# First layer's tokens come turned, and their 1/rms is applied behind the projections

## What is computed

```python
def _rms_norm(x, g):
    y = xf * lax.rsqrt(jnp.mean(xf * xf, axis=-1, keepdims=True) + NORM_EPS)
    return (y * g.astype(jnp.float32)).astype(x.dtype)

h = _rms_norm(x, norm_mix)
proj = h @ w_in                       # 1024 x 3336
rq, rk, rv, rg, fq, fk, fv, fl, cb, cc, ch = jnp.split(proj, split_at, axis=-1)
# A: retention: rotary on rq, rk; values rv; group norm and swish gate rg
# B: forgetting attention: RMS norm of each head of fq, fk; logf = log_sigmoid(fl + bias)
u = cc * ch
y_conv, new_conv = _causal_dwconv(u, conv_hist, conv_w)
o_conv = (cb * y_conv).astype(x.dtype)
x = x + jnp.concatenate([o_ret, o_fox, o_conv], axis=-1) @ w_out
h2 = _rms_norm(x, norm_ffn)
x = x + (jax.nn.silu(gate_c) * (h2 @ w_up)) @ w_down
```

## Time and profile before

| | us |
|---|---|
| Median of 3 runs | 1559.53 (1558.76 to 1560.35) |
| Span of the profiled execution | 1557.5 |
| PE busy | 1538.9 |
| DVE busy | 1056.6 |
| ACT busy | 661.2 |
| POOL busy | 408.5 |
| First 128x512 product of the projections | at 11.58 |
| First forget-gate matmul (end of chunk 0) | at 45.20 |

### The profile page before, as it was taken

The page is one execution under the profiler, slowest core; times in us unless marked ns, Lnnn a source line. Parts: engine busy times, 40 slices in busy tenths (PEclk is TensorE's granted clock), DMA queues, the critical chain, the costliest instruction groups (busy, mean ns, idle before and its releaser), DMA issues.

```text
span 1557.5 us, 28313 instructions
## 1 busy us (share of the span) xinstructions
PE 1538.9 (99%) x9860; PEld 1343.1 (86%) x9860; DVE 1056.6 (68%) x1805; ACT 661.2 (42%) x1236; POOL 408.5 (26%) x513
## 2 busy tenths in 40 slices
PE   8999999999999999999999999999999999999998
PEld 6878896789999999999888788867899999999997
DVE  4446447449988788888644563574599887888885
ACT  4223337336544444444333133373364444444441
POOL 1113210004433333333112041100145333333330
PEclk9999999999999999999999999999999999999999
DMA  7213436531322222222242235465223222222222
GB/s 235 82 49 94 140 122 239 211 95 55 108 82 85 85 85 83 85 88 68 80 109 68 71 85 168 145 235 178 68 90 100 81 81 81 81 81 81 81 69 85
DMA packets 116971, 163.80 MB, mean 105 GB/s; under 512 B 28049, under 2 KB 80401, under 8 KB 112802
## 3 DMA queue, kind: packets, MB, share of 16 engines
q1 hardware_dynamic: 116752, 162.75, 33.1%
q10 hardware_dynamic: 146, 0.07, 0.0%
HBM read 152.91 MB, written 9.63 MB: 104 GB/s over the span
## 4 chain that ended last, share of the span: by engine, by line
PE 93%; DVE 3%; ACT 1%; DMA 1%; issue 1%; POOL 0%; POOLq 0%; DVEq 0%; SPq 0%; ACTq 0%
PE bank L2233 89%; PE bank L2295 4%; DVE pf L1884 0%; DMA raw<-in_w_gate 0%; DVE pf L1897 0%; DVE xn L1572 0%; DMA raw<-in_w_in 0%; DVE x L2008 0%; DVE wlo L1534 0%; POOLq L1110 0%; POOL s L1108 0%; DVE gulo L1544 0%; ACT xn L1216 0%; POOL small L978 0%; DVE xlo L1534 0%
## 5 line engine op out<-in xcount | busy, mean ns | idle before, releaser
L2233 PE MATMUL bank<-whi,hhi 128*128 128x512 f32 x560 | 226.0, 404 | 0.9 <-DVE hlo L1544 0.6
L2233 PE MATMUL bank<-whi,hlo 128*128 128x512 f32 x560 | 219.4, 392 | 0.0
L2233 PE MATMUL bank<-wlo,hhi 128*128 128x512 f32 x560 | 219.0, 391 | 0.0
L2233 PE MATMUL bank<-hhi,whi 128*128 128x320 f32 x640 | 198.7, 310 | 0.8 <-DVE hlo L1544 0.8
L2233 PE MATMUL bank<-hhi,wlo 128*128 128x320 f32 x640 | 197.8, 309 | 0.0
L2233 PE MATMUL bank<-hlo,whi 128*128 128x320 f32 x640 | 197.6, 309 | 0.0
L2233 PE MATMUL bank<-whi,guhi 128*128 128x512 f32 x440 | 171.9, 391 | 0.2
L2233 PE MATMUL bank<-wlo,guhi 128*128 128x512 f32 x440 | 171.3, 389 | 0.0
L2233 PE MATMUL bank<-whi,gulo 128*128 128x512 f32 x440 | 171.3, 389 | 0.0
L1520 DVE TENSOR_TENSOR wlo<-raw,whi 128x1024 fp32r<-128x1024 f32 x80 | 100.1, 1251 | 99.7 <-ACT whi L1143 98.1
L2008 DVE TENSOR_TENSOR x<-x,bank 128x512 f32<-128x512 f32 x220 | 142.8, 681 | 29.6 <-PE bank L2233 29.2
(11 more groups left out here) (307 smaller groups left out, 3500.6 us busy)
## 6 DMA issues: line engine op xcount, KB each, us to landing
raw<-in_w_in SPq DMA_DIRECT2D x52, 512.0 KB, 3.8
raw<-in_w_gate SPq DMA_DIRECT2D x44, 512.0 KB, 3.8
raw<-in_w_down SPq DMA_DIRECT2D x44, 512.0 KB, 3.6
raw<-in_w_up SPq DMA_DIRECT2D x24, 512.0 KB, 3.8
vb<-in_cache_fox_v SPq DMA_DIRECT2D x10, 1024.0 KB, 5.5
gains<-in_w_up SPq DMA_DIRECT2D x20, 512.0 KB, 3.7
raw<-in_w_out SPq DMA_DIRECT2D x16, 512.0 KB, 4.6
bcr<-scr_p SPq DMA_DIRECT2D x8, 512.0 KB, 5.0
```

Of the source, the lines that this page charges most:

```text
L2233: return pe.matmul(out, lhsT=lhsT, rhs=rhs, start=start, stop=stop, skip_group_check=True)
```

## The change

In layer 0 the host also gives the tokens turned (`x_turned`, with the first layer's gain in eight columns ahead). ACT rounds x^T times the gain straight into `hhi` (`hi(k)`), DVE makes the rest (`rest(k)`), for k = 0 to 7, with 640 tokens in each. There is no norm and no transpose ahead of the products; slab 0 is used by row, k = 0 for all tiles, then k = 1, and its two halves are loaded by ACT's queue. The row sums and 1/rms are made afterwards from x, which is loaded later. The 1/rms of a token is then applied where the projections are read: as the scale of ACT's copies and Silu, on the rotary's cos and sin, on the forget values, through the epsilon of the head norms (`FLOOR`), and for the turned branch (cc, ch, cb) as a row `rb`, which SP sends through DRAM (`scr_r`) to all partitions: POOL multiplies cc with its square and y with itself. Layer 1 runs as before. The diff, cut:

```diff
+        rb = own("rb", [P, NTOK])
+        (xt, fqT, fkT, fv, h11, h12, guhi, gulo, gact, t2h, t2l, s1, s2) = region(
+            [("xt", [P, XT], F32)],
...
-            load_x(sp, 0)
-            sp.dma_start(const[:, 0:P], a["c_tables"][:, 0:P]).then_inc(ident_in, 16)
...
-                    sp.wait_ge(lo_split, nth(n, l))
+                    if l > 0 or n >= SLOTS:
...
+            def load_xt(i):
+                c0, c1 = (KT + NTOK * k if k else 0 for k in XT_PARTS[i:i + 2])
+                sp.dma_start(xt[:, c0:c1], a["x_turned"][:, c0:c1]).then_inc(xt_in[i], 16)
+
+            load_xt(0)
+            load_xt(1)
+            load(1, 0, slab_src(1, 0))
+            load_xt(2)
+            load(2, 0, slab_src(2, 0))
+            load_xt(3)
+            load_xt(4)
+            load(SLOTS, 0, slab_src(SLOTS, 0))
+            sp.dma_start(const[:, :], a["c_tables"]).then_inc(consts_in, 16)
...
+                if l == 0:
+                    for t in range(3):
+                        load_x(sp, t)
...
+                if l == 0:
+                    sp.wait_ge(rstd, TT)
+                    sp.dma_start(scr_r.rearrange("t p -> p t"), small[:, RS:RS + TT], allow_slow_non_contiguous=True).then_inc(r_out, 16)
+                    sp.wait_ge(r_out, 16)
+                    sp.dma_start(rb[:, :], bass.AP(scr_r.tensor, 0, [[0, P], [1, NTOK]])).then_inc(rb_in, 16)
 
...
+            turned_before = [sum(1 for t in range(TT) for g in range(2) if B.bank(("hT", 0, t, g)) == b) for b in range(8)]
             for b in range(8):
-                pool.sem_inc(B.free[b], 1)
+                pool.sem_inc(B.free[b], 1 + turned_before[b])
+                if turned_before[b]:
+                    pool.sem_inc(B.full[b], turned_before[b])
+            pool.sem_inc(h_hi, 2 * TT)
+            pool.sem_inc(xn_ready, TT)
             pool.sem_inc(lo_split, SLOTS)
             pool.sem_inc(x_done, 2 * TT)
...
+                    if l == 0 and which == 0:
+                        pool.tensor_scalar(col(FLOOR + t), col(VAR + t), EPS, 0.0, ALU.mult, ALU.add)
...
+                if l == 0:
+                    pool.wait_ge(rb_in, 16)
+                    pool.tensor_tensor(rb2[:, :], rb[:, :], rb[:, :], ALU.mult)
+                    pool.drain()
...
+                for i in range(4) if l == 0 else ():
+                    ft, half = i // 2, i % 2
+                    hs = slice(half * HALF, half * HALF + HALF)
+                    B.wait_taken(pool, ("cc_", ft, half), l)
+                    pool.tensor_tensor(ccs[:, ft, hs], ccs[:, ft, hs], rb2[:, hs], ALU.mult).then_inc(cc_scaled, 1)
...
+                for ft in range(2) if l == 0 else ():
+                    pool.wait_ge(y_conv, ft + 1)
+                    apart(pool)
+                    pool.tensor_tensor(ycv[:, ft, 0:SEQ], ycv[:, ft, 0:SEQ], rb[:, 0:SEQ], ALU.mult)
+                    rows = ycv[:, ft, NY - NB * (NS + 2):NY].rearrange("p (b s) -> p b s", b=NB)[:, :, 2:]
+                    pool.tensor_tensor(rows, rows, rb[:, SEQ:].rearrange("p (b s) -> p b s", b=NB), ALU.mult)
+                    pool.drain().then_inc(y_scaled, 1)
...
-            act.dma_start(vb[0:1, 0, 0:2, :].rearrange("p k n -> p (k n)"), a["norm_mix"][bass.ds(0, 1)]).then_inc(gains_in, 16)
+            def turned_tokens(l):
+
+                def hi(k):
+                    if k in XT_PARTS:
+                        act.wait_ge(xt_in[XT_PARTS.index(k)], 16)
+                    act.activation(hhi[:, k, :], xt[:, KT + NTOK * k:KT + NTOK * (k + 1)], ACT.Copy,
+                                   scale=xt[:, k:k + 1]).then_inc(xt_hi, 1)
+
+                hi(0)
+                act.wait_ge(w_first_in, 16)
+                act.activation(whi[:, 0, 0:512], raw[:, 0, 0:512], ACT.Copy).then_inc(w_first_hi, 1)
+                hi(1)
+                wait_loaded(act, 0, l)
+                act.activation(whi[:, 0, 512:], raw[:, 0, 512:], ACT.Copy).then_inc(hi_split, 1)
+                split_to[0] = 1
+                upto(1, l)
+                hi(2)
+                hi(3)
+                upto(2, l)
+                for k in range(4, KT):
+                    hi(k)
+                upto(3, l)
+
+            def token_squares():
+                for t in range(TT):
+                    act.wait_ge(x_in[t], 16)
+                    if t >= 2:
+                        act.wait_ge(rstd, t - 1)
+                    act.activation(rT[:, 2 * (t % 2):2 * (t % 2) + 2, 0:512], x[:, t, :].rearrange("p (c n) -> p c n", c=2), ACT.Square,
+                                   accum_out=col(SS + t)).then_inc(sumsq, 1)
+                    if t == 1:
+                        upto(FL, 0)
+                    if t == 2:
+                        upto(FL + 1, 0)
+
+            for k, done in ((0, w_first_in), (1, raw_in[0])):
+                act.dma_start(raw[:, 0, 512 * k:512 * k + 512].rearrange("p (k n) -> p k n", k=1),
+                              a["w_in"][bass.ds(0, 1)].rearrange("o (k p) n -> p (o k) n", p=P)[:, k:k + 1, 0:512]).then_inc(done, 16)
...
-                norm(0, l, {0: 0, 1: 2} if l == 0 else {0: 0, 2: 1, 3: 2})
+                if l == 0:
+                    turned_tokens(l)
+                    token_squares()
+                else:
+                    norm(0, l, {0: 0, 2: 1, 3: 2})
...
+                    act.activation(gs[:, t, :], bk[:, 256:512], ACT.Silu, scale=token_scale(t)).then_inc(silu_ready, 1)
+                    act.activation(rv[:, t, :], bk[:, 0:256], ACT.Copy, scale=token_scale(t)).then_inc(B.free[B.bank(("c", 1, t))], 1)
...
-            dve.wait_ge(gains_spread, 1)
-            dve.tensor_copy(gains[:, 0:512], bank[6][:, :])
-            dve.drain()
-            dve.wait_ge(ident_in, 16)
+            def turned_tokens(l):
+
+                def rest(k):
+                    dve.wait_ge(xt_hi, k + 1)
+                    dve.scalar_tensor_tensor(out=hlo[:, k, :], in0=xt[:, KT + NTOK * k:KT + NTOK * (k + 1)], scalar=xt[:, k:k + 1],
+                                             in1=hhi[:, k, :].bitcast(F32), op0=ALU.mult, op1=ALU.subtract).then_inc(xt_lo, 1)
+
+                rest(0)
+                dve.wait_ge(w_first_hi, 1)
+                lo(wlo[:, 0, 0:512], raw[:, 0, 0:512], whi[:, 0, 0:512]).then_inc(w_first_lo, 1)
+                rest(1)
+                dve.wait_ge(hi_split, 1)
+                lo(wlo[:, 0, 512:], raw[:, 0, 512:], whi[:, 0, 512:]).then_inc(lo_split, 1)
+                split_to[0] = 1
+                upto(1, l)
+                rest(2)
+                rest(3)
+                upto(2, l)
+                for k in range(4, KT):
+                    rest(k)
...
+                    csr = cs[:, t]
+                    if l == 0:
+                        dve.wait_ge(rstd, t + 1)
+                        csr = wcn[:, 64 * (t % 2):64 * (t % 2) + 64].rearrange("p (s d) -> p s d", s=2)
+                        dve.tensor_scalar(csr, cs[:, t], col(RS + t), None, ALU.mult)
...
-                    B.wait_taken(dve, ("cc_", i // 2, i % 2), l)
+                    if l == 0:
+                        dve.wait_ge(cc_scaled, i + 1)
+                    else:
+                        B.wait_taken(dve, ("cc_", i // 2, i % 2), l)
...
                 def conv_times(ft, half):
                     key = ("cb_", ft, half)
+                    if l == 0:
+                        dve.wait_ge(y_scaled, ft + 1)
...
-            pe.wait_ge(gains_in, 16)
-            for c in range(2):
-                mm(bank[6 + c][:, :], ob[0:1, 0, :], vb[0:1, 0, c, :], True, True).then_inc(gains_spread, 1)
-            pe.wait_ge(ident_in, 16)
...
+                def slab_by_row():
+                    pe.wait_ge(w_first_lo, 1)
+                    for k in range(2):
+                        pe.wait_ge(xt_lo, k + 1)
+                        if k == 1:
+                            ready(0, l)
+                        for t in range(TT):
+                            key, ts = ("c", 0, t), slice(t * P, t * P + P)
+                            if k == 0:
+                                B.wait_room(pe, key, l)
+                            ins = mm3(bank[B.bank(key)][:, :], hhi[:, k, ts], hlo[:, k, ts], whi[:, 0, 512 * k:512 * k + 512],
+                                      wlo[:, 0, 512 * k:512 * k + 512], k == 0, False)
+                    ins.then_inc(slab_used, 1)
+
...
-                norm(0, l, first_slabs)
-                first_slabs(TT)
-                chunk0(2, l, range(1 if l == 0 else 0, TT))
-                chunk0(3, l)
+                if l == 0:
+                    slab_by_row()
+                    for i in (1, 2, 3):
+                        pe.wait_ge(xt_lo, 2 * i + 2)
+                        chunk0(i, l)
+                    pe.wait_ge(consts_in, 16)
+                else:
+                    norm(0, l, first_slabs)
+                    first_slabs(TT)
+                    chunk0(2, l)
+                    chunk0(3, l)
```

(39 more changed lines are left out.)

96 lines of the change are left out of this document (41 added, 55 removed).

## The result

The changed kernel takes 1550.65 us (median of 4 runs, 1550.01 to 1551.51) against 1559.24 us for the kernel before, timed beside it (1558.76 to 1560.35): a ratio of 0.9944, interval 0.9932 to 0.9956, and 8.6 us less. The forecast was 1550.8 us. The profiled execution spans 1549.7 us, 7.8 less than before.

What follows compares the result with a forecast made beforehand. PE was taken as the bound. Chunk 0 ending 9.1 us earlier (4.7 start, 4.4 transposes), less 0.4 given back, makes 8.7 us: 1559.5 to 1550.8 us, range 1548 to 1555.

Steps and rivals of the forecast that it cites:

- What bounds the kernel: Whole kernel: PE, busy 99%, sets the pace; time gained before 45.20 us should arrive at the end.
- The start: First product in layer 0: at 6.9 us instead of 11.58, bounds 6.4 to 7.75, a gain of 4.7 us.
- The transposes: Between chunk 0's products: transposes of token tiles 1 to 4 take 4.4 us of PE, which go.
- The lower level: First products of chunk 0: running at the 1.2 GHz level costs 2.0 us, kept unchanged, bounds 2.0 either way.
- slow-start rival: Start of chunk 0: 30 products at the lower level cost 6.0 us instead of 2.0; 1555.7 us; chance 0.08.
- Is PE fed: Chunk 0: each token piece and slab is ready 3 us or more before PE wants it.
- Given back: Layer 0's mixer: Pool working beside DVE slows fox_scale(0), costing 0.4 us, bounds 0 and 2.
- there DVE has nothing to spare: At fox_scale(0): it ends at 224.5 us and PE's transposes of its result start at 224.59.
- The sum: Whole kernel: chunk 0 ends 9.1 us earlier, 0.4 given back, so 8.7 us less.
- The round trip of 1/rms: SP's write and broadcast read through scr_r: about 4 us with both issues, hidden.
- The rival "slower": SP's scr_r round trip eats the gain from 13.1 us on; at 20 us the time is 1566.4; chance 0.04.
- The scalings on Pool: Layer 0's convolution branch: four cc products at 1.3 us each, hidden; ycv about 2.7 us per tile.

Runs made afterwards that it cites:

- e3: Changed kernel with 32 dead transposes put back on PE in four groups of eight between the products of chunk 0; 1554.39 us, ratio 0.9969.
- e1: The changed kernel run once more with no edit; 1550.82 us, ratio 0.9947.
- e5: Changed kernel with the first weight slab's halves issued by SP behind the first and second token pieces, instead of by ACT; 1550.37 us, ratio 0.9941.
- e2: Changed kernel with two extra fp32 matmuls of 512 columns on zeros on PE ahead of the first product; 1549.39 us.
- e9: Changed kernel with two extra fp32 matmuls of 512 columns on ones on PE ahead of the first product; 1548.94 us.
- e6: Changed kernel with all five x tiles loaded ahead of slab 1 instead of behind slab 3; 1553.27 us, ratio 0.9961.
- after: The changed kernel itself, in its first profiled execution; span 1549.7 us, median of its runs 1550.65 us.
- e7: Changed kernel with sixteen dead Pool products of 160 columns ahead of each of the two scalings of ycv; 1572.97 us, ratio 1.0095.

## Why the prediction was right

**What bounds the kernel.** Right. Nearly all that was gained ahead of 45.20 arrived at the end: 8.15 us at chunk 0, 7.8 at the span, and in e3 chunk 0 later by 4.4 than e1 with the span later by 4.3.

**The start: 6.9 forecast, 7.27 measured (7.16 to 7.60 over the executions with this start).** The chain had the forecast's links in its order. Two terms were small: the xt piece came to ACT at 4.72 and not 4.5, and ACT's 640 columns took 0.83 us, 0.84 in the chain, where scaling 0.577 by columns gave 0.72. The rest(0) of 0.89 and wlo of 0.69 were right. The claim that two queues move what one moves held for the sum of the pieces, but not for the first: it could have been there at 3.83 (e5).

**The transposes: 4.4 forecast.** Right as a sum, 33.6 less the products and the lower level; e3 and the first two old groups split it into 3.5 of transposes and 0.9 of waiting. The 4.4 was a remainder, and a remainder holds the waits too.

**The lower level: kept at 2.0, measured 2.5.** Within its bounds. By 120 x 0.227 = 27.2 it is 1.4 us in one execution (e1) and 2.5 in another of the same program; in the kernel before, with 8 products, it was 1.9 by the starts (11.58 to 15.47). The Trainium skill ("TensorE: Matmul & The Clock Gate", Part 1) says that the number of products at the lower level varies from run to run; the trace agrees, with 6 to 14. The slow-start rival, 30 products at 0.43, did not occur in any. The four matmuls that went had not raised the level in the profiled execution, nor had their like in those of e2 and e9; the times of e9's other executions leave room for it.

**Is PE fed: right.** No wait inside chunk 0. e6 shows that this hangs on the order of the loads.

**Given back: 0.4 forecast, 0.25 to 0.35 measured, at another place.** The size was about right and the place wrong. Pool beside DVE does make fox_scale(0) 0.12 us slower, but the step "there DVE has nothing to spare" failed: PE's transposes already followed the preceding matmul without a stop, and 0.12 us fits between. What was given back came for the most part at the second norm, where Pool's 1/rms is 0.2 us late, a place that the prediction did not look at. That the two sizes agree is luck.

**The sum: 8.7 forecast.** The profiled spans differ by 7.8: chunk 0 gave 8.15 instead of 9.1 (0.4 us for the start, 0.6 for the lower level), and 0.35 came back. The medians differ by 8.6, closer than the terms deserve: the profiled execution is the slowest of its four, with twelve products at the lower level. e1, the same program with six fewer, spans 1548.9, which is 8.6 less than before.

**The round trip of 1/rms: about 4 us forecast, 14.5 measured, hidden all the same.** Timeline of SP in after:

```profile
111.07 0.46 SPq L834 DMA_DIRECT2D scr_r<-small  x1
121.42 0.34 SPq L836 DMA_DIRECT2D rb<-scr_r  x1
```

The 2.5 KB write had its receipt after 10.3 us, and the read of rb took 4.1 more. That is not time spent behind other loads: the last slab issued ahead of it landed at 116.11, and the windows from 115 to 121 us print a DMA share of 0.00. The row for small pieces, 2.9 us, was the wrong neighbour: it is a read of 32 KB. The place had slack enough: cc's first scaling comes at 187.22. The rival "slower" had its deciding point at 13.1 us of blocked SP; the measured 10.3 + 0.5 came nearer to it than its chance of 0.04 says, yet PE waited for nothing behind it.

**The scalings on Pool.** Forecast at 1.3 us each for cc and 2.7 for a tile of ycv; 0.88 and 1.7 to 2.0 measured. DVE's idle time ahead of the first convolution product is 6.06 us, as in the earlier trace rows: hidden, as forecast. The lead of 3.9 us was not worked out in the prediction; e7 shows that it decides.

## What to carry to other kernels

Where PE is the bound, count what its own line holds before the first product and between the first ones, and test the remainder: part of it may be waiting. Put the piece that everything waits for alone on the transfer engines until it has landed, and order the rest by the time at which PE wants it. Before moving work to a helper engine, work out how long before its reader it finishes; here 3.9 us of lead cost nothing, and using up that lead cost the stall and then a stretch at the lower clock level on top.

## What the runs showed of the hardware

- In the profiled executions, twenty bf16 matmuls of 256 columns ahead of the first product left none (ones, 3.87 us, ended 0.4 us before it) or one (zeros, 4.45 us, up to it) of the products at the lower level; two fp32 matmuls of 512 columns (3.78 us) left nine, on zeros and on ones alike. Six of the seven other fp32 executions took 1548.4 to 1549.4 us, as the bf16 ones did (1547.8 to 1549.6), so that fp32 matmuls never raise the level is not shown.
- After PE had stood for 7.65 and for 3.92 us in e7, its products started 0.267 us apart instead of 0.147, and the granted clock of those windows is printed as 0.68 and 0.57. At the start of after it is printed as 1.00 over twelve products at 0.43 us. The spacing is the safer reading.
- A DRAM write of 2.5 KB, 640 values of 4 B, took 10.3 us to its receipt, the last 5 of them with no other load in flight.
- A piece of 332 KB on one queue landed 0.9 us later (4.70 instead of 3.81) with two pieces of 256 KB issued beside it on a second queue than with the same pieces behind it on its own.
- ACT's rounding copy of 640 columns with a scale per row took 0.83 us, and 0.51 for 256.
